# Second mixing of a two-block model: smaller products for three of seven levels, a shorter diagonal, and exponentials placed ahead of the value copy

## The reference, cut to what matters

```python
q, f_raw, i_in, g_out, b_gate, c_gate, x_conv, gate_a, gate_b = split(u @ w_in)
q = silu(q)
f = lb + (1.0 - lb) * sigmoid(f_raw)      # one lower bound lb for each key channel
logf = log(f);  k = 1.0 - f;  v = i_in
# per head and chunk: G = cumsum(logf)
diff = G[:, :, :, None, :] - G[:, :, None, :, :]
decay = exp(where(causal, diff, -inf))
A = sum(q[t] * k[s] * decay[t, s], axis=-1)     # s <= t
o = (q * exp(G)) @ S + A @ v                    # S: state carried from chunk to chunk
o = rmsnorm(o) * silu(g_out)
merged = sigmoid(gate_a) * o + sigmoid(gate_b) * b_gate * conv(c_gate * x_conv)
```

## Time and profile before

| | |
|---|---|
| median of 3 runs | 1885.07 us (1881.64 to 1885.74) |
| the profiled execution | 1887.12 us, of which the span is 1885.3 us |
| TensorE matmuls busy | 1810.8 us, 96% of the span, 11324 records |
| VectorE busy | 1036.7 us, 55% |
| ScalarE busy | 532.1 us, 28% |
| GpSimd busy | 1459.1 us, 77% |
| second mixing | about 926 to 1460 us of the span |

### The profile page before, as it was taken

How to read it: one execution, slowest core, us unless ns; L and a number is a source line. 1 busy time by engine, 2 the same in 40 slices (tenths; PEclk the granted TensorE clock), 3 DMA queues, 4 the chain that set the end, 5 groups by cost and what they waited for, 6 DMA issues and landing times.

```text
span 1885.3 us, 33496 instructions
## 1 busy us (share of the span) xinstructions
PE 1810.8 (96%) x11324; PEld 1589.1 (84%) x11324; DVE 1036.7 (55%) x1675; ACT 532.1 (28%) x784; POOL 1459.1 (77%) x2245
## 2 busy tenths in 40 slices
PE   4999997999999999999899999999999999999997
PEld 2767774568799999888799999999999999999885
DVE  6447987645767666611556555555664355555101
ACT  3236662220122111100433443443443211111000
POOL 2758982359999999999567766776775899999885
PEclk8899997999999999999999999999999999999999
DMA  8332232334522222333122222222221223223332
GB/s 323 96 116 87 95 118 82 119 111 135 177 90 89 89 90 90 99 111 100 57 78 76 71 68 77 70 69 68 78 79 57 90 89 97 92 89 100 100 100 89
DMA packets 54300, 184.43 MB, mean 98 GB/s; under 512 B 6673, under 2 KB 7857, under 8 KB 54226
## 3 DMA queue, kind: packets, MB, share of 16 engines
q1 hardware_dynamic: 48690, 169.20, 28.6%
q10 hardware_dynamic: 5536, 14.16, 2.2%
HBM read 178.62 MB, written 4.72 MB: 97 GB/s over the span
## 4 chain that ended last, share of the span: by engine, by line
PE 53%; POOL 27%; issue 12%; DMA 2%; DVEq 2%; DVE 1%; ACT 1%; POOLq 1%; SPq 1%; ACTq 0%
POOL Wlo L370 16%; PE gp L379 16%; PE gp L380 16%; PE gp L381 16%; POOL Whi L367 7%; POOL probe L366 4%; PE A L681 3%; DMA raw<-units 2%; DVEq L1465 2%; DMA AW<-ada 1%; PE A L710 0%; PE A L729 0%; DVE XX L1463 0%; SPq L315 0%; PE A L731 0%
## 5 line engine op out<-in xcount | busy, mean ns | idle before, releaser
L370 POOL TENSOR_TENSOR Wlo<-raw,Whi 128x256 fp32r<-128x256 f32 x1120 | 964.7, 882 | 46.8
L379 PE MATMUL gp<-XNhi,Whi 128*128 128x264 f32 (+3 forms) x2736 | 849.4, 310 | 27.7 <-DVE XNlo L1074 23.8
L380 PE MATMUL gp<-XNlo,Whi 128*128 128x264 f32 (+3 forms) x2736 | 836.0, 306 | 0.0
L381 PE MATMUL gp<-XNhi,Wlo 128*128 128x264 f32 (+3 forms) x2736 | 833.2, 305 | 0.0
L379 PEld LDWEIGHTS gp<-XNhi,Whi 128*128 128x128 f32 x2736 | 518.2, 189 | 65.2 <-POOL Wlo L370 17.6
L380 PEld LDWEIGHTS gp<-XNlo,Whi 128*128 128x128 f32 x2736 | 518.4, 189 | 24.8 <-issue 2.2
L381 PEld LDWEIGHTS gp<-XNhi,Wlo 128*128 128x128 f32 x2736 | 517.6, 189 | 23.3
L366 POOL TENSOR_TENSOR probe<-raw 1x1 f32<-1x1 f32 x560 | 172.3, 308 | 358.2 <-PE gp L381 316.3
L367 POOL TENSOR_SCALAR Whi<-raw 128x512 fp32r<-128x512 f32 x560 | 347.0, 620 | 0.0
L379 PE MATMUL gp<-AChi,Whi 128*128 128x512 f32 x352 | 139.3, 396 | 0.1
L380 PE MATMUL gp<-AClo,Whi 128*128 128x512 f32 x352 | 139.0, 395 | 0.0
(11 more groups left out here) (302 smaller groups left out, 2222.0 us busy)
## 6 DMA issues: line engine op xcount, KB each, us to landing
raw<-units SPq DMA_DIRECT2D x280, 512.0 KB, 3.5
AW<-ada SPq DMA_DIRECT2D x16, 512.0 KB, 8.8
AWL<-ada SPq DMA_DIRECT2D x16, 512.0 KB, 4.2
AWL<-ada ACTq DMA_DIRECT2D x16, 512.0 KB, 4.5
bias_rows<-RB ACTq DMA_DIRECT2D x1, 2560.0 KB, 15.5
H<-xT SPq DMA_DIRECT2D x1, 2048.0 KB, 9.3
BIAS<-bias_rows ACTq DMA_DIRECT2D x1, 2048.0 KB, 9.6
out<-H SPq DMA_DIRECT2D x8, 256.0 KB, 2.1
```

Source lines behind the costliest of these rows:

```text
L370: ins = pool.tensor_tensor(lo[:, c:c + UNIT // 4], src[:, c:c + UNIT // 4], hi[:, c:c + UNIT // 4].bitcast(F32), ALU.subtract)
L379: pe.matmul(dst, Whi[s][:, k, :], rhi, start=start, stop=False)
L380: pe.matmul(dst, Whi[s][:, k, :], rlo, start=False, stop=False)
L381: return pe.matmul(dst, Wlo[s][:, k, :], rhi, start=False, stop=stop)
```

## The change

Four things change.

- For b = 64 and 32 (levels 0 and 1) the product of a chunk no longer has all 128 columns as weights. It takes for each block of 2b only the b lower columns as weights and the b upper columns as the moving operand, and writes b partitions of PSUM. That is one product of 64x64 for a chunk of level 0 and two of 32x32 for a chunk of level 1.
- For b = 1 (level 6) the factor between neighbours is exp(logf) of the odd position. `boundary(6)` goes, ScalarE computes one exponential from HL, VectorE multiplies q by it and then k by that (the second waits for the first), and TensorE sums it over the channels with one product with ones as weights over 264 columns, in place of five products. The count of `d_ready` falls from 8 to 7 per head.
- The diagonal is summed over columns 112 to 640 only, and k = 1 - f is computed in one VectorE instruction in place of two (a negated column LAM[:, 3] is prepared once).
- On ScalarE `decay(0)` and `decay(1)` stand ahead of the copy of the value.

```diff
 def level(l):
     b = LEVELS[l]
     pe.wait_ge(lx_ready, i * 18 + hh * 9 + l + 2)
     if l >= 2:
         pe.wait_ge(lev_out, i * 16 + hh * 8 + l - 1)
-    for c in range(first_chunk(l), CH):
+    o = A45[:, (l % 2) * 512:(l % 2) * 512 + CH * 64]
+    if b == 1:
+        mm = pe.matmul(o[:, PAD // 2:], ones, XX[:, l % 2, PAD // 2:CH * 64], start=True, stop=True)
+    for c in range(first_chunk(l), CH if b > 1 else 0):
         x = XX[:, l % 2, c * P:(c + 1) * P]
+        if b >= 32:
+            for j in range(P // (2 * b)):
+                r = 2 * b * j
+                mm = pe.matmul(o[r:r + b, c * 64 + b * j:c * 64 + b * (j + 1)], x[:, r:r + b], x[:, r + b:r + 2 * b],
+                               start=True, stop=True)
+            continue
         up = x.rearrange("p (j two b) -> p j two b", two=2, b=b)[:, :, 1, :]
-        mm = pe.matmul(A45[:, (l % 2) * 512 + c * 64:(l % 2) * 512 + (c + 1) * 64], x, up,
-                       start=True, stop=True)
+        mm = pe.matmul(o[:, c * 64:(c + 1) * 64], x, up, start=True, stop=True)
     mm.then_inc(lev_mm, 1)
...
-for a, w in ((0, 512), (512, TP - 512)):
+for a, w in ((PAD, 512 - PAD), (512, TP - 512)):
     mm = pe.matmul(A67[:, a:a + w], ones, XX[:, 1, a:a + w], start=True, stop=True)
...
 act.activation(HQ[:, PAD:TP], ps, ACT.Silu).then_inc(free, 1)
 act.drain().then_inc(hq_ready, 1)
+decay(0, LEVELS[0])
+decay(1, LEVELS[1])
 ps, free = psum(2)
 act.wait_ge(hv_mm, h + 1)
 act.activation(HVT[:, PAD:TP], ps, ACT.Copy).then_inc(free, 1)
 act.drain().then_inc(hvt_ready, 1)
-decay(0, LEVELS[0])
-decay(1, LEVELS[1])
...
-decay(6, LEVELS[6])
+act.wait_ge(lx_ready, i * 18 + hh * 9 + 6)
+act.activation(EE[:, 0, 0:CH * 64].rearrange("p (t o) -> p t o", o=1),
+               HL[:, :].rearrange("p (t two) -> p t two", two=2)[:, :, 1:2], ACT.Exp).then_inc(e_ready, 1)
...
-dve.tensor_scalar(HK[:, PAD:TP], HF[:, PAD:TP], LAM[:, 6, bass.ds(h, 1)], LAM[:, 5, bass.ds(h, 1)],
-                  ALU.mult, ALU.add).then_inc(f_ready, 1)
-dve.drain()
-dve.tensor_scalar(HK[:, PAD:TP], HK[:, PAD:TP], -1.0, 1.0, ALU.mult, ALU.add)
+dve.tensor_scalar(HK[:, PAD:TP], HF[:, PAD:TP], 1.0, LAM[:, 3, bass.ds(h, 1)], ALU.subtract,
+                  ALU.mult).then_inc(f_ready, 1)
...
 dve.wait_ge(e_ready, i * 16 + hh * 8 + l + 1)
+if b == 1:
+    q, k = [t[:, :].rearrange("p (t two) -> p t two", two=2) for t in (HQ, HK)]
+    f, x = [t[:, 0, 0:CH * 64].rearrange("p (t o) -> p t o", o=1) for t in (EE, XX)]
+    dve.tensor_tensor(f, q[:, :, 1:2], f, ALU.mult)
+    dve.drain()
+    dve.tensor_tensor(x, k[:, :, 0:1], f, ALU.mult)
+    dve.drain().then_inc(lx_ready, 1)
+    return
...
 for l in range(len(LEVELS)):
     weigh(l)
-    if l + 2 < len(LEVELS):
+    if l + 2 < len(LEVELS) - 1:
         boundary(l + 2)
```

More of the change, by code:

```diff
@@ L976, in decay @@
                     def decay(l, b):
-                        act.wait_ge(d_ready, i * 16 + hh * 8 + l + 1)
+                        act.wait_ge(d_ready, i * 14 + hh * 7 + l + 1)
                         n = i * 18 + hh * 9 + l
@@ L1016, in _ @@
                     act.drain().then_inc(side_ready, 1)
-                    decay(6, LEVELS[6])
+                    act.wait_ge(lx_ready, i * 18 + hh * 9 + 6)
+                    act.activation(EE[:, 0, 0:CH * 64].rearrange("p (t o) -> p t o", o=1),
+                                   HL[:, :].rearrange("p (t two) -> p t two", two=2)[:, :, 1:2], ACT.Exp).then_inc(e_ready, 1)
                     act.activation(EG[:, P:TP], HG[:, P:TP], ACT.Exp).then_inc(eg_ready, 1)
-                    act.wait_ge(d_ready, i * 16 + hh * 8 + 8)
+                    act.wait_ge(d_ready, i * 14 + hh * 7 + 7)
                     act.wait_ge(lx_ready, i * 18 + hh * 9 + 8 + 1)
@@ L1216, in _ @@
             dve.tensor_scalar(LAM[:, 0, :], pl, 8.0, None, ALU.mult)
+            dve.tensor_scalar(LAM[:, 3, :], LAM[:, 6, :], -1.0, None, ALU.mult)
             dve.drain().then_inc(lam_done, 1)
```

## The result

The changed kernel took 1860.16 us (median of 4 runs, 1858.17 to 1864.59) against 1885.4 us before (median of 4). The ratio is 0.9864, with a 95% interval from 0.9843 to 0.9886. Measured again beside 17 executions of the kernel before, it took 1861.55 us, with the ratio 0.9860 (0.9831 to 0.9890).

The account below looks back on a forecast made before the run. TensorE's own work was taken to bound the kernel. Gains of 1.03 (levels 0 and 1), 0.62 (level 6) and 0.19 (diagonal) made 1.84 us per head, 14.7 for eight, so 1870.4 us against the 1885.07 median; range 1863 to 1878.

Parts of the forecast that it names:

- The wait at level 1: TensorE's wait for VectorE in each head, 1.03 us idle, was to vanish with 2 us to spare.
- Levels 0 and 1: Their TensorE time per head was to fall from 3.03 to 2.00 us, a gain of 1.03.
- the tiny transposes: Four transposes in the trace, 0.068 us apart, the shortest distance seen; 0.061 per narrow record was taken as nearest to it.
- the low bound of 0.027: Level 1 on TensorE: the lowest price in us per record, if a record shrinks with its weight columns.
- the rival of cheap products: Levels 0 and 1: records shrink with their weight columns, 2.54 us gained per head, 1865 us in all; chance 0.16.
- The serial rival: Levels 0 and 1: each narrow record runs by itself at 0.272 us, 3.2 us lost per head, 1911; chance 0.05.
- The changes of width: Levels 0 and 1 on TensorE: three changes of product width per head were to cost 0.53 us in all.
- the narrow products only break even: Levels 0 and 1: 1.70 us now against 2.00 then, so the gain of 1.03 is just the old wait.
- Level 6: On TensorE ten records of 1.06 us become two of 0.44 in all, a gain of 0.62 per head.
- The diagonal: Four records, 1.14 us on TensorE; two lose 112 of 512 columns, a gain of 0.19 us per head.
- k and LAM: The single VectorE instruction for k and the once-prepared column LAM[:, 3] were to cost nothing on TensorE.
- The sum: All gains per head, 1.03 + 0.62 + 0.19 = 1.84 us, 14.7 us for eight heads.

Follow-up runs that it names:

- experiment 1: Kernel before with only decay(0) and decay(1) moved ahead of the copy of the value: 1872.93 us, ratio 0.9937.
- experiment 2: Changed kernel with decay(0) and decay(1) put back behind the copy of the value: 1869.79 us, ratio 0.9921.
- experiment 3: Kernel before with only the products of levels 0 and 1 narrowed: 1878.71 us, ratio 0.9971.
- experiment 7: Changed kernel with level 1 issued first for output partitions 0 to 31, then for 64 to 95, not in turn: 1863.30 us, ratio 0.9879.
- experiment 9: Changed kernel with levels 2 to 5 as two products of 64 x 32 for a chunk: 1852.27 us, ratio 0.9808.
- experiment 10: Changed kernel with levels 0 to 5 all in products of 32 weight columns: 1841.02 us, ratio 0.9763.
- experiment 6: Changed kernel with levels 0 and 1 issued chunk by chunk, nine width changes in place of three: 1868.88 us, ratio 0.9915.
- experiment 4: Changed kernel with the full 128x64 products put back for levels 0 and 1: 1862.58 us, ratio 0.9887.
- experiment 5: Kernel before with only level 6 as a row sum and the diagonal over 528 columns: 1880.34 us, ratio 0.9964.
- experiment 8: Changed kernel with level 0 as two products of 32 x 64 for a chunk: 1859.69 us, ratio 0.9861.

## Why the prediction was wrong

The direction, the bound and the vanishing wait were right. The size was off because one term, the cost of a record of level 1, was four times too large.

**The wait at level 1.** Right. It was to vanish with 2 us to spare, and vanished with 2.5. The order of ScalarE did it alone (experiment 1), and without it neither the narrow products nor the shorter k could (experiments 2 and 3).

**Levels 0 and 1.** This step failed: "I take 0.061 for both, nearest to the tiny transposes: 8 records 0.49 and 16 records 0.98." Level 0 is right, 8 records at 0.057 or 0.46. The sixteen records of level 1 took 0.24, not 0.98, at 0.0147 each, below even the low bound of 0.027. Two things were wrong in the one term. The larger is the record by itself: in one output group it costs 0.032 (experiment 7), not 0.061. That is 0.46 us of the missing 0.74 per head. I had carried over the distance of the tiny transposes, a row of another shape; why those are 0.061 to 0.085 apart no run shows. The other is the overlap: two products that write different groups of partitions run at the same time, 0.0147 in place of 0.032, the other 0.28 us. The low bound had left it out. The row that I held against the rival of cheap products (the gaps around L562) measured the change of width, not the record.

The prediction also said that no record in the trace is closer to the next than 0.068. That is a misreading. In the first block of the kernel before stand products whose operands lie in turn in the lower and the upper 64 partitions, and their records start in pairs 0.006 us apart. Two of 0.48 us each take 0.49 together, and later pairs follow 0.21 us apart, which by 0.432 for 512 columns is the estimated price of one such record alone:

```profile
91.36 0.49 PE L478 MATMUL A<-KI,QI 64*128 64x256 f32 x2
```

They differ in the half of the input partitions and not of the output, but they did show, before any run, that products in different parts of the array can run side by side.

What came true is the rival of cheap narrow products, to which the prediction gave a chance of 0.16. It had 2.54 us per head and 1865, against the measured 2.75 and 1860; it lacked the overlap, 0.19 us (0.43 for level 1, where 0.24 was measured).

The serial rival had looked at exactly this place, the output in turn to the lower and the upper half, and put the wrong sign on it: the turns are what makes them cheap. The Trainium skill had it right where I did not look: TensorE: Matmul & The Clock Gate (Part 3, row and column tiling) says that matmuls in different 32x32 tiles of the array run concurrently, and that the tile's column goes by where the output starts in PSUM; experiments 7, 9 and 10 agree. The same page (Part 1) says that matmuls never start less than about 25 ns apart. In one output group that fits the 32 ns of experiment 7; across four groups 72 and 80 records started about 9 ns apart in a row, and the measurement decides.

**The changes of width.** Right. Three were to cost 0.53. Measured are 0.09 ahead of level 0 and 0.40 behind it (1.09 less 0.46 and 0.24), 0.49 in all, and experiment 6 gives 0.13 for one more. This agrees with the drain at a change of mode in the Trainium skill, TensorEngine Tiling (Array Packing), Key Properties.

**Levels 0 and 1 in sum** gave 1.85 us per head (3.03 to 1.09, less 0.09), not 1.03. The difference is 6.6 us over eight heads. The statement that the narrow products only break even was wrong: they are worth 0.63 us per head (experiment 4), where full ones without a wait take 1.79. Its sum had slips too: beside 1.70 and the wait of 1.03, 0.30 of the 3.03 remains and not 0.33, and full records of these levels are 0.112 apart (1.79 / 16), not 0.106.

**Level 6** was to gain 0.62 and gained 0.62. **The diagonal** was to gain 0.19 and gained 0.24. Both are confirmed alone in experiment 5. k and LAM cost nothing that a head shows.

**The sum** was to be 1.84 per head and 14.7 in all; it is 2.75 and 22.0. The rest up to the measured 25 is inside the interval of the ratio, which reaches down to 21.5. In the two profiled executions the difference is larger, 27.4 us of span (1885.3 to 1857.9), and their traces show where it lies. The heads give 22.0. The first transposes start 2.4 us later before (940.2 to 937.8); that is ahead of the mixing, and the changed kernel and its repeat differ there by 3.1 (937.8 and 940.9). From the start of the eighth transposes (1406.0 and 1384.3) to the end it is 479.3 us before and 473.6 after, 5.7 less, of which the eighth head is 2.75. The other 3.0 is two falls of the clock that the profile of before has and that of the changed kernel does not.

One is the fall behind the wait at level 1, at 1410, some 1.5 us. The change can claim it, if it comes that often: it came four times in the four profiles that have the wait, one per execution on average, and in none of the ten others. That is argued from few profiles.

The other does not belong to the change. Behind the last head TensorE waits some 1.8 us for VectorE in every kernel, and in 7 of the 14 profiles the clock falls behind it, with the wait at level 1 or without. The changed kernel and its repeat differ by it (first the repeat: the wait, then a window behind it, with the granted clock third from the end, at its low level; then the same place in the first profile, at the full one):

```profile
1437.12 0.36 PE L379 MATMUL gp<-M2hi,Whi 128*128 128x258 f32 x1 [1.78 <-DVE M2lo L1566]
1439.00:1440.00 1.00, 1.00 (x7) 1.00 (x7) 0.00 (x0) 0.97 (x2) 0.92 (x3) 0.50 0.00 0
...
1434.04 0.36 PE L379 MATMUL gp<-M2hi,Whi 128*128 128x258 f32 x1 [1.78 <-DVE M2lo L1566]
1436.00:1437.00 1.00, 1.00 (x11) 1.00 (x10) 0.00 (x0) 1.00 (x2) 1.00 (x2) 1.00 0.00 0
```

From the start of the eighth transposes to the end the repeat takes 475.0 us and the first profile 473.6, so this fall costs 1.5 too. How often either fall comes in the executions without a profile, and with it what the 25 us of the medians consist of beyond 22.0, stays open.

## What to carry to other kernels

When small products are bound by their weight loads, cut the weights in groups of 32 columns whose outputs lie in different groups of 32 partitions, and issue them in turn. Four times the products then cost less than half the time (72 records in 0.87 us against 18 in 2.01), but keep one width for as long as possible, since each change costs about 0.13 us. Look first at what an in-order engine has queued ahead of the critical instructions: putting four exponentials ahead of one copy was worth more (10 us) than the narrow products that were placed with it (5 us). To bound a shape that a trace does not have, ask what can run beside it, not only how long one of it is, and look in the whole trace for records that start together.

## What the runs showed of the hardware that I had not expected

- Records of plain fp32 matmuls with 32 weight columns and 32 moving ones start 0.032 us apart in one output group and 0.0147 in two; with 16 moving columns they start about 0.009 apart in four groups, over 80 records. With 64 weight columns they start 0.057 apart in one group (64 moving) and 0.030 in two (32 moving). Within one group the wider side counts in these traces: 0.058 for 64 weight and 32 moving columns (experiment 9), 0.056 for 32 and 64 (experiment 8).
- An idle time of TensorE of 1.05 to 1.2 us between two groups of small products was followed, behind 4 of 32 such waits, by a stretch at the low clock that cost another 1.5 us. Idle times of the same length, and up to 1.40 us, had nothing behind them. The idle time of 1.78 us behind the last head had such a stretch behind it in 7 of 14 profiles.
